# Small block inverses on TensorE: 64x64 quarters against 32x32 tiles on the array's diagonal

## The reference

```python
c = GDN_CHUNK                                   # 64
a_mat = beta[..., :, None] * jnp.einsum('nhcid,nhcjd->nhcij', k, k) * d_strict
rhs = jnp.concatenate([beta[..., None] * v, (beta * gam)[..., None] * k], axis=-1)
sol = lax.linalg.triangular_solve(a_mat, rhs, left_side=True, lower=True, unit_diagonal=True)
u0, w = sol[..., :dv], sol[..., dv:]
...
def step(s, inp):
    w_c, u0_c, p_c, qg_c, kd_c, ge_c = inp
    u = u0_c - jnp.einsum('nhcd,nhde->nhce', w_c, s)
    o = jnp.einsum('nhcd,nhde->nhce', qg_c, s) + jnp.einsum('nhij,nhje->nhie', p_c, u)
    s = ge_c[..., None, None] * s + jnp.einsum('nhcd,nhce->nhde', kd_c, u)
```

## Time and profile before

| | |
|---|---|
| median of 3 runs | 2622.61 us (2614.13 to 2623.71) |
| the profiled execution's own time | 2623.43 us |
| its span | 2621.6 us |
| PE busy | 2040.8 us, 78% of the span |
| DVE, ACT busy | 796.9 us, 582.3 us |
| `product` (L453), MATMUL records | 6656, busy 224.6 us |
| mean granted clock | 0.869 of 2.4 GHz |

### The profile page before, as it was taken

One profiled execution on the slowest core, in us unless ns is written; L12 is line 12 of the kernel. 1 busy time (PEld: TensorE's weight loads), 2 busy tenths in 40 slices (PEclk: granted clock), 3 DMA queues, 4 the chain that ended last, 5 costly groups with the idle time before them and its releaser, 6 DMA issues.

```text
span 2621.6 us, 46011 instructions
## 1 busy us (share of the span) xinstructions
PE 2040.8 (78%) x18624; PEld 1159.7 (44%) x18624; DVE 796.9 (30%) x1522; ACT 582.3 (22%) x980; POOL 172.6 (7%) x239
## 2 busy tenths in 40 slices
PE   5997673877777735968886879897968886879896
PEld 1444242444444412547735722443547835822442
DVE  1207312111111123435427513411435426513401
ACT  2115220000000002242224222401242124222401
POOL 0000002111111100001003000000001003000000
PEclk8998785999999977979888876998979798875998
DMA  9342011999999951100000020011100000020010
GB/s 354 134 176 97 18 64 40 370 419 417 414 413 414 418 222 49 58 25 3 3 4 2 25 77 0 1 64 50 58 25 3 3 5 2 25 77 0 1 64 32
DMA packets 80130, 303.57 MB, mean 116 GB/s; under 512 B 8748, under 2 KB 20252, under 8 KB 54736
## 3 DMA queue, kind: packets, MB, share of 16 engines
q1 hardware_dynamic: 70464, 287.75, 27.9%
q0 software_dynamic: 5872, 9.68, 1.1%
q10 hardware_dynamic: 3616, 3.59, 0.4%
HBM read 296.67 MB, written 12.71 MB: 118 GB/s over the span
## 4 chain that ended last, share of the span: by engine, by line
PE 69%; DVE 11%; another core or an unknown queue 10%; ACT 5%; issue 3%; ACTq 0%; DVEq 0%
PE bank L433 15%; PE bank L1868 9%; PE bank L453 5%; PE bank L1884 4%; PE bank L853 4%; PE bank L1663 3%; PE bank L1819 2%; PE bank L1717 2%; PE bank L819 1%; DVE arena L1267 1%; ACT arena L863 1%; PE bank L446 1%; PE bank L833 1%; PE bank L1680 1%
## 5 line engine op out<-in xcount | busy, mean ns | idle before, releaser
L433 PE MATMUL bank<-hT,arena 128*128 128x512 f32 (+2 forms) x896 | 400.9, 609 | 20.1 <-remote 20.1
L1868 PE MATMUL bank<-arena 128*64 128x256 f32 x2048 | 245.4, 396 | 89.0 <-remote 89.0
L433 PEld LDWEIGHTS bank<-hT,arena 128*128 128x128 f32 (+2 forms) x896 | 170.4, 191 | 248.3 <-issue 248.3
L453 PE MATMUL bank<-arena 64*64 64x64 f32 x6656 | 224.6, 227 | 47.3 <-DVE arena L1261 26.8
L453 PEld LDWEIGHTS bank<-arena 64*64 64x64 f32 x6656 | 214.8, 142 | 57.7 <-DVE arena L1261 28.3
L1868 PEld LDWEIGHTS bank<-arena 128*64 128x64 f32 x2048 | 152.0, 142 | 194.8 <-issue 137.0
L863 ACT ACTIVATE arena<-bank 128x512 f32<-128x512 f32 (+4 forms) x158 | 93.4, 591 | 269.9 <-PE bank L433 134.5
L2318 DVE COPY arena<-bank 128x256 f32<-128x256 f32 x32 | 13.6, 425 | 393.5 <-PE bank L1876 393.5
L1884 PE MATMUL bank<-arena 128*64 128x512 f32 x512 | 116.9, 598 | 17.1 <-remote 17.1
L853 PE MATMUL bank<-arena 128*128 128x512 f32 x256 | 112.1, 600 | 4.4 <-remote 4.4
L1663 PE MATMUL bank<-sq,c_sb 128*128 128x512 f32 (+1 forms) x116 | 70.2, 740 | 40.0 <-ACT sq L870 28.8
(11 more groups left out here) (374 smaller groups left out, 2681.1 us busy)
## 6 DMA issues: line engine op xcount, KB each, us to landing
arena<-w_gate SPq DMA_DIRECT2D x32, 2048.0 KB, 15.6
arena<-w_up SPq DMA_DIRECT2D x32, 2048.0 KB, 20.2
arena<-w_down SPq DMA_DIRECT2D x32, 2048.0 KB, 11.4
arena<-w_ada SPq DMA_DIRECT2D x12, 2048.0 KB, 19.7
arena<-w_in SPq DMA_DIRECT2D x10, 2048.0 KB, 8.3
arena<-w_out SPq DMA_DIRECT2D x6, 2048.0 KB, 7.9
arena<-w_in SPq DMA_DIRECT2D x6, 1536.0 KB, 7.2
arena<-y_scratch SPq DMA_DIRECT2D x4, 1024.0 KB, 11.3
```

The lines of the kernel that those rows point to most:

```text
L433: m = pe.matmul(bank[b][lo:lo + w, :], slot2(n)[:, k, c:c + w], hT[:, k, :], start=(k == 0), stop=(k == KD - 1))
L453: m = pe.matmul(o[half(f), s, t], lhs[half(f), s, t], rhs[half(f), s, t], start=True, stop=True)
L1868: mm = pe.matmul(bank[b][c * CAP:(c + 1) * CAP, 0:FE // 2], XT[j][:, k % 4, k // 4, :], slot(ring_at + i)[:, k, c * (FE // 2):(c + 1) * (F ...
```

## The change

The products of levels 1 to 4 go to a new function, `small_product`, which multiplies only the 32x32 blocks on the diagonal of each chunk matrix: for each head and token tile four matmuls of 32x32x32, on partitions 32q to 32q + 31 for q = 0 to 3, each on the array tile at rows and columns 32q. Level 5 and all other calls keep `product`. What lies outside the diagonal blocks in a bank is no longer written in these levels; ACT and DVE read the same whole tiles as before, and the masks of levels 1 to 4 take nothing from there.

```diff
+            def small_product(b, lhs, rhs):
+
+                o, lhs, rhs = pieces(bank[b]), pieces(lhs), pieces(rhs)
+                for s in range(2):
+                    for t in range(TT):
+                        for q in range(4):
+                            rows, cols = slice(32 * q, 32 * q + 32), slice(32 * (q % 2), 32 * (q % 2) + 32)
+                            m = pe.matmul(o[rows, s, t, cols], lhs[rows, s, t, cols], rhs[rows, s, t, cols], start=True, stop=True)
                 return m
...
-                            product(d, g_Bn[d], g_T[d]).then_inc(sem(f"g_v_done{d}"), 1)
+                            (small_product if l < LEVELS - 1 else product)(d, g_Bn[d], g_T[d]).then_inc(sem(f"g_v_done{d}"), 1)
...
                             if l < LEVELS - 1:
-                                product(2 + d, g_Y[d], g_V[d]).then_inc(sem(f"g_t_done{d}"), 1)
+                                small_product(2 + d, g_Y[d], g_V[d]).then_inc(sem(f"g_t_done{d}"), 1)
                             else:
                                 product(2 + d, g_V[d], g_Y[d]).then_inc(sem(f"g_t_done{d}"), 1)
...
-                            product(d, r_Bn[d], r_bt[:, ct, d]).then_inc(sem(f"g_v_done{d}"), 1)
+                            (small_product if l < LEVELS - 1 else product)(d, r_Bn[d], r_bt[:, ct, d]).then_inc(sem(f"g_v_done{d}"), 1)
...
                             if l < LEVELS - 1:
-                                product(2 + d, Y, V).then_inc(sem(f"g_t_done{d}"), 1)
+                                small_product(2 + d, Y, V).then_inc(sem(f"g_t_done{d}"), 1)
```

More of the change, by code:

```diff
@@ L454, in product @@
                 return m
+            def small_product(b, lhs, rhs):
[5 more added lines that the diff above has]
+                            m = pe.matmul(o[rows, s, t, cols], lhs[rows, s, t, cols], rhs[rows, s, t, cols], start=True, stop=True)
+                return m
             def gdn_chunks():
```

## The result

The change made the kernel slower: 2735.34 us (2732.18 to 2739.06, 4 runs) against 2619.92 us (2614.13 to 2623.71, 4 runs), a ratio of 1.0434 with a 95% interval of 1.0407 to 1.0461. The forecast was 2592 us.

The account below looks back on a forecast made before the run. A ring of TensorE and DVE was taken to bound most levels; savings of 15.1 (GDN levels 2 to 4), 6.7 and 1.7 (RWKV) and 7.2 (GDN level 1) sum to 30.7 us, giving 2592 us, range 2583 to 2614.

Parts of the forecast that it names:

- costs of nothing: Items priced at zero: products under DVE's part, passages between tile sizes, and 10,240 more instructions on top of 37,248.
- gaps on TensorE with no releaser: Sign listed as showing the forecast wrong through instructions: TensorE idle with nothing in the profile that it waited for.
- The ring: V 1, T product 0 and DVE's copy 0, transpose 0, copy 1 in turn: 4.29 us a level, forecast to become 3.45.
- The price of the small product: TensorE, one 32x32-tile product: 16 turns of 34 ns, 0.54 us in place of 0.94, saving 0.42 with latency.
- the walk through its cold products: GDN level 1, starting at clock 0.50: 0.85 us a product; 1.8 and 1.0 us saved in two blocks, 1.2 taken.
- The fastest row's 14.4 ns a record: Rival: TensorE can start records no faster, so only latency is gained, 2621 us, or half way 2607; chance 0.17.
- The passages between tile sizes: Two a block, before the first V and before V 0 of level 5, where TensorE waits anyway; no cost.
- The clock rival: TensorE's clock falls to 1.2 GHz in the levels: chance 0.05 slower, 0.08 for a part (gain 10 to 20 us).
- its worse case: Clock low through the levels, level 5 and the quarters behind: +2.5 us a block, +20 us, 2643 us; chance 0.05.
- the rival's 0.6 us: Added to a 3.45 us level at 1.2 GHz, making 4.1 us, still 0.2 under the level before.
- The first RWKV block: First of each layer: DVE sets levels of 5 us and more; only level 1 gains, 1.7 us in all.
- The two floors: TensorE: a 29.3 ns price per record, 64 us slower, chance 0.03; row tiles taking turns on a bank, over 70 slower.

Follow-up runs that it names:

- e7: Kernel before the change, with two of four token tiles left out in levels 2 to 4 of both mixers, on 64x64 quarters: 2591.18 us against 2622.18.
- e8: Kernel before the change, with 32x32 tiles for one head of T product 0, levels 2 to 4 (GDN, second RWKV block): 2619.26 us against 2621.01.
- e3: Kernel before the change, with each 64x64 matmul doubled into a spare bank in levels 1 to 4 of GDN, no 32x32 tiles: 2692.1 us.
- e2: Changed kernel, with small products doing only one of four token tiles in levels 2 to 4, 128 TensorE instructions a level: 2599.96 us.
- e4: Kernel before the change, with small products only for V of direction 1 and T product of direction 0, levels 1 to 4, both mixers: 2660.65 us.
- e5: Kernel before the change, with small products only in level 1 of GDN: 2627.70 us against 2622.18, ratio 1.0018.
- e6: Kernel before the change, with small products only in level 1 of GDN, T product 1 there kept full: 2628.14 us, ratio 1.0018.
- e9: Kernel before the change, with 32x32 tiles for both heads of T product 0, levels 2 to 4 (GDN, second RWKV block): 2625.25 us, ratio 1.0015.

## Why the prediction was wrong

**The step that failed** is the one that put instructions among the costs of nothing: "a level after the change needs two in 3.45 us. I find no wait for it." The packets' own 0.95 us was nearly right (1.05 on average before, 1.10 after). Wrong was to take it for the period: two packets in the levels are 3.3 to 4.3 us apart, 3.7 on average, so a level of two pieces takes 7.3. The trace of before had the warning. A level used just one piece in 4.29 us, so that the supply was about 80% taken without a wait to be seen, and no two packets in that trace were ever closer than 3.31 us. The sum of durations says how busy a queue is; how fast it can be asked is rather to be read from the least distance between its packets. The prediction's last paragraph named the sign, gaps on TensorE with no releaser, but gave it neither a price nor a chance of its own.

**The ring** was right, and so was what it does with a shorter product: e7 takes 0.94 us from a level by two halved products, 3.36 us, and its blocks are 22 us shorter.

**The price of the small product** was right: turns of 31 to 32 ns at full clock where I took 34, 64 records in 0.84 us with their latency at a mean clock of 0.81, and level 1 of GDN in 3.43 us in four blocks of six, as the walk through its cold products gave (3.41). The other two, 4.39 and 4.83, waited for a piece. The fastest row's 14.4 ns a record was no limit of starting.

**The passages between tile sizes** were priced at nothing with TensorE's waits as cover. In the changed kernel that is not contradicted, since it pauses there anyway; e8 shows 0.1 to 0.15 us for one on the ring.

**The clock rival** (0.05 and 0.08) came true in its first half: the clock was 0.50 in the levels of all ten blocks, but for 0.74 in level 2 of two. The changed kernel came out slower, as its worse case says, but not by the clock: e3 has the same 7.2 us a level at 1.00, because TensorE waits for instructions anyway. What the clock would cost in a level without that wait, the rival's 0.6 us, no run shows. My reason against it, that TensorE would "earn the clock back", was wrong: in e2 the clock stayed at 0.50 through levels that follow each other at 2.88 us. With supply out of the way it would have cost part of the gain: 1.5 us from level 4 to level 5 in e2, the figure of the rival.

**The first RWKV block**, where DVE set a level at 5.4 us, was forecast to be safe. It lost too, to 7.36, for two pieces of instructions outlast DVE's work as well.

**The two floors** (a price per record, and a bank used by one row tile at a time) did not show: starts 7 ns apart in one bank, and a turn of 32 ns for four tiles, speak against both.

What stays open: what asks for the next piece, and what fills the 3.3 to 4.3 us between two. The packets' starts, 1.1 to 1.6 us after a burst's, fit a request made when TensorE enters the last piece it holds; no run changed that. Why the clock falls with the small tiles is open too, and how much of the 6.6 us outside the blocks is more than the spread between runs.

## What to carry to other kernels

Count instructions per microsecond beside busy time. A stream of small matmuls that is cut in half doubles its instructions, and in this kernel TensorE can be fed 256 of them (two for each MATMUL record) in about 3.6 us; a stretch that needs more, beyond the 270 to 510 that lie ready after a wait, pauses with no releaser in the profile, however short its matmuls. Here, with 256 instructions in 4.3 us, a finer tile could only pay if the number of matmuls hardly grew, and none of the partial versions (e4, e5, e6, e8, e9) was faster than the kernel before.

## What the runs showed of the hardware

- Instructions reach TensorE in packets of 16 KB, 256 instructions; the least distance between two is 3.0 to 3.4 us in every run here, and 3.7 on average in the levels of the changed kernel and of e3, although one takes 0.9 to 1.7. At most about two pieces lie ready: after a wait of 4.5 us 508 instructions ran without a pause in two blocks of e5, and 274 in two of e6. The Trainium skill (Runtime: NRT & Kernel Launch, Instruction fetch mechanics) describes blocks of 256 that are fetched while the current one runs, and calls this hidden; the trace agrees on the block and on the fetch during the run (1.1 to 1.6 us into a burst), and not on its being hidden.
- Four 32x32 tiles on the diagonal work at once: a turn of 31 to 32 ns for the four, a start every 8 ns, in one bank (e8).
- At the same number of records and nearly the same busy time (514 and 518 in 15 us, 8.56 and 8.87 us), the granted clock was 0.50 with 32x32 tiles and 1.00 with 64x64 quarters.
